# Order and size of attention's loads, and the order in which the attention result is split, in a one-layer encoder step

## The reference, cut to what matters

```
h = rmsnorm(x) * (1 + scale) + shift            # shift, scale, gate from silu(c) @ w_ada + b_ada
q, k, v, indexer, z_a, z_b, g_a, g_b = split(h @ w_in)     # q, k get a per-head RMS norm
att_a = attention over the top-k keys that an indexer picks (8 heads, 2 kv heads, dim 64)
att_b = attention over own chunk of 64 and 2 before it, with a sink per head
o_a = (att_a * silu(z_a)) @ w_oa ;  o_b = (att_b * silu(z_b)) @ w_ob
y = x + gate * ((sigmoid(g_a) * o_a + sigmoid(g_b) * o_b) @ w_out)
```

## Time and profile before

| | |
|---|---|
| time before, median of 3 (lowest to highest) | 1013.48 us (1010.45 to 1014.51) |
| the profiled execution's own time | 1018.09 us |
| its span, first to last instruction | 1016.3 us |
| PE busy / weight loads busy | 959.4 us (94%) / 855.6 us (84%) |
| DVE / ACT / POOL busy | 652.5 us (64%) / 392.3 us (39%) / 375.1 us (37%) |
| mean granted TensorE clock | 0.973 of full |
| DMA | 126.40 MB, 124 GB/s on the mean |

### The profile page before, as it was taken

One profiled execution on the slowest core, in us unless ns is written; L12 is line 12 of the kernel. 1 busy time (PEld: TensorE's weight loads), 2 busy tenths in 40 slices (PEclk: granted clock), 3 DMA queues, 4 the chain that ended last, 5 costly groups with the idle time before them and its releaser, 6 DMA issues. The chain is left out here.

```text
span 1016.3 us, 17645 instructions
## 1 busy us (share of the span) xinstructions
PE 959.4 (94%) x6482; PEld 855.6 (84%) x6482; DVE 652.5 (64%) x1375; ACT 392.3 (39%) x1166; POOL 375.1 (37%) x420
## 2 busy tenths in 40 slices
PE   4859999999999999999999888999999889999998
PEld 2558887878789999999999666778777679999998
DVE  6563365999999999999980575766665553331111
ACT  5664566444422322122111555666665522212100
POOL 0261113212253533121243477655631145537332
PEclk9878999999999999999999798999999899999999
DMA  9820013643461323232132834423334665534332
GB/s 319 305 73 28 25 34 108 227 162 94 141 205 59 115 82 108 81 107 76 63 136 71 252 97 139 140 91 102 96 102 111 196 189 163 152 93 139 101 121 73
DMA packets 112187, 126.40 MB, mean 124 GB/s; under 512 B 12105, under 2 KB 89305, under 8 KB 111978
## 3 DMA queue, kind: packets, MB, share of 16 engines
q1 hardware_dynamic: 101698, 114.30, 36.2%
q10 hardware_dynamic: 10408, 11.01, 3.5%
HBM read 95.49 MB, written 35.75 MB: 129 GB/s over the span
## 5 line engine op out<-in xcount | busy, mean ns | idle before, releaser
L1569 PE MATMUL PS<-HH,WH 128*128 128x384 f32 (+1 forms) x576 | 188.8, 328 | 0.0
L1571 PE MATMUL PS<-HH,WL 128*128 128x384 f32 (+1 forms) x576 | 187.9, 326 | 0.0
L1570 PE MATMUL PS<-HL,WH 128*128 128x384 f32 (+1 forms) x576 | 187.7, 326 | 0.0
L1404 DVE MAX8 M<-SC 128x8 f32<-128x384 f32 (+3 forms) x210 | 174.8, 870 | 11.6 <-DVE SC L1409 11.0
L1409 DVE MATCH_REPLACE8 SC<-M,SC 128x384 f32<-128x384 f32 (+3 forms) x210 | 179.9, 864 | 0.0
L880 POOL TENSOR_TENSOR WL<-RAW,WH 128x512 fp32r<-128x512 f32 x72 | 94.2, 1312 | 182.0 <-ACT WH L1031 182.0
L1569 PE MATMUL PS<-WH,HH 128*128 128x512 f32 (+3 forms) x288 | 111.1, 386 | 8.6 <-DVE HL L1348 8.5
L1569 PEld LDWEIGHTS PS<-HH,WH 128*128 128x128 f32 x576 | 108.1, 188 | 3.8 <-issue 3.7
L1570 PE MATMUL PS<-WL,HH 128*128 128x512 f32 (+3 forms) x288 | 109.0, 378 | 0.0
L1571 PE MATMUL PS<-WH,HL 128*128 128x512 f32 (+3 forms) x288 | 108.7, 377 | 0.0
L1570 PEld LDWEIGHTS PS<-HL,WH 128*128 128x128 f32 x576 | 108.1, 188 | 0.0
(11 more groups left out here) (202 smaller groups left out, 1967.4 us busy)
## 6 DMA issues: line engine op xcount, KB each, us to landing
RAW<-in_w_all SPq DMA_DIRECT2D x72, 256.0 KB, 2.7
gz<-STG SPq DMA_DIRECT2D x48, 192.0 KB, 1.8
WADA<-in_w_ada SPq DMA_DIRECT2D x16, 512.0 KB, 12.3
snat<-STG SPq DMA_DIRECT2D x24, 256.0 KB, 2.0
QKV<-snat SPq DMA_DIRECT2D x8, 768.0 KB, 5.7
GT<-gz SPq DMA_DIRECT2D x32, 192.0 KB, 2.5
XN<-in_x_prompt SPq DMA_DIRECT2D x8, 512.0 KB, 6.1
btad<-bvd ACTq DMA_DIRECT2D x4, 1024.0 KB
```

What stands on the lines that cost most here:

```text
L1404: V.max(M8[0:r, a, :], w).then_inc(sel_step, 1)
L1569: T.matmul(out, wh, mh, start=first, stop=False)
L1570: T.matmul(out, wh, ml, start=False, stop=False)
L1571: return T.matmul(out, wl, mh, start=False, stop=last)
```

## The change

Four things. (1) Of attention's first loads only `BTB` and `VB` stay ahead of the loop; `BTA`'s first piece and `VA` go to SP's step 1, the six loads for the sample to step 9, and the gate of group 0 is loaded at step -1 instead of 4. (2) A tile's `QKV` is loaded 14 steps ahead instead of 7. (3) The rest of `BTA` comes in two pieces of 256 and 512 columns (1 MB and 2 MB), issued by ScalarE at steps 13 and 36, instead of six pieces of 128 columns issued by SP at steps 13, 35, 51, 67, 83 and 99. (4) `AZ` has both halves of column group 0 first; ScalarE's third high part moves from step 137 to 139, and DVE's second, third and fourth low part are made at step 139 and behind the loop, where the second was at step 135 and the third at 139.

```
--- before.py
+++ after.py
@@ -408,7 +408,7 @@
         U8 = 16 * SAMPLE
         GEND = [max(u for u, x in enumerate(UNITS) if x[:2] == (g // 2, g % 2)) + 1 for g in range(2 * NT)]
 
-        AZ = [(0, 0), (1, 0), (0, 1), (1, 1), (2, 0), (2, 1)]
+        AZ = [(0, 0), (0, 1), (1, 0), (1, 1), (2, 0), (2, 1)]
 
         def nh(tt):
 
@@ -463,11 +463,10 @@
         assert all(TQ[n][1] == ("Q", 0, n) for n in range(EARLY_T))
         PREP0 = {16 * (tt - 1): tt for tt in range(NT)}
         CACHE_STEP = {16 * (2 + i): i for i in range(5)}
-        LOAD_AT, NORM_AT, SPLIT_AT = -7, -5, 2
+        LOAD_AT, NORM_AT, SPLIT_AT = -14, -5, 2
         RD_AT, RB_AT, FIN_AT = ({GEND[g] + d: g for g in range(2 * NT)} for d in (1, 4, 4))
         ZR_AT, OUT_AT = ({GEND[g] + (d if g < 2 * NT - 1 else e): g for g in range(2 * NT)} for d, e in ((8, 6), (9, 7)))
-        BT_AT = {13 if tt == 2 else 16 * (tt - 1) + 3: tt for tt in range(2, SAMPLE)}
-        ZT_AT = {GEND[g] + (2 if g == 2 * NT - 1 else 0 if g // 2 == SAMPLE else -4): g for g in range(2 * NT)}
+        ZT_AT = {GEND[g] + (2 if g == 2 * NT - 1 else 0 if g // 2 == SAMPLE else -9 if g == 0 else -4): g for g in range(2 * NT)}
         SINK_AT = {GEND[2 * tt + 1]: tt for tt in range(NT)}
 
         def prep(s, after):
@@ -717,13 +716,6 @@
 
             sp.dma_start(BTB[:], btbd).then_inc(kvb_in, 16)
             sp.dma_start(VB[:], vp[:, :, 1408:1536]).then_inc(kvb_in, 16)
-            sp.dma_start(BTA[:, :, 768:1024], btad[:, :, 768:1024]).then_inc(kvc_in, 16)
-            sp.dma_start(VA[:], vp[:, :, 640:768]).then_inc(kvc_in, 16)
-            for dst, src in ((CK[:, 0:4, :], t["cache_ak"].rearrange("(n p) c -> p n c", p=128)), (CK[:, 4, :], t["cache_bk"]),
-                             (VAS[:, 0:4, :], t["cache_av"].rearrange("(n p) c -> p n c", p=128)),
-                             (VAS[0:DEC, 4, :], snat[SEQ:TOK, 640:768]),
-                             (VBS[:, 0, :], t["cache_bv"]), (VBS[0:DEC, 1, :], snat[SEQ:TOK, 1408:1536])):
-                sp.dma_start(dst, src).then_inc(rest_in, 16)
             for i in range(3):
                 sp.wait_ge(stg_out[i], 16 * NST[i])
             wo_v = t["w_o"].rearrange("(k p) n -> p k n", p=128)
@@ -748,11 +740,15 @@
                 if s == NU + 1:
                     sp.wait_ge(exp_done, NU)
                     g_load(0)
-                if s in BT_AT:
-                    tt = BT_AT[s]
-                    if tt >= 3:
-                        sp.wait_ge(min_done, 16 * (tt - 1) + 1)
-                    sp.dma_start(BTA[:, :, 896 - 128 * tt:1024 - 128 * tt], btad[:, :, 896 - 128 * tt:1024 - 128 * tt]).then_inc(bta_in, 16)
+                if s == 1:
+                    sp.dma_start(BTA[:, :, 768:1024], btad[:, :, 768:1024]).then_inc(kvc_in, 16)
+                    sp.dma_start(VA[:], vp[:, :, 640:768]).then_inc(kvc_in, 16)
+                if s == 9:
+                    for dst, src in ((CK[:, 0:4, :], t["cache_ak"].rearrange("(n p) c -> p n c", p=128)), (CK[:, 4, :], t["cache_bk"]),
+                                     (VAS[:, 0:4, :], t["cache_av"].rearrange("(n p) c -> p n c", p=128)),
+                                     (VAS[0:DEC, 4, :], snat[SEQ:TOK, 640:768]),
+                                     (VBS[:, 0, :], t["cache_bv"]), (VBS[0:DEC, 1, :], snat[SEQ:TOK, 1408:1536])):
+                        sp.dma_start(dst, src).then_inc(rest_in, 16)
                 tt = prep(s, LOAD_AT)
                 if tt is not None and tt >= 2:
                     sp.wait_ge(xg_ready, tt - 1)
@@ -1190,6 +1186,11 @@
                 nc.scalar.dma_start(ZST[g][:], attd.rearrange("(k p) n -> p k n", p=128)[:, :, g0:g0 + gn]).then_inc(z_in[g], 16)
 
             for s in range(S0, S1):
+                if s in (13, 36):
+                    c = slice(512, 768) if s == 13 else slice(0, 512)
+                    if s == 36:
+                        act.wait_ge(min_done, 33)
+                    nc.scalar.dma_start(BTA[:, :, c], btad[:, :, c]).then_inc(bta_in, 16)
                 if s == U8 - 12:
                     act.wait_ge(xg_ready, NT)
                     z_load(0)
@@ -1243,7 +1244,7 @@
                     tt = SINK_AT[s]
                     act.wait_ge(sink_sum, tt + 1)
                     nc.scalar.activation(ES[:, 0, :], SD[:], ACT.Exp).then_inc(sink_act, 1)
-                if s == NU + 1:
+                if s == NU + 3:
                     act.wait_ge(min_done, NU)
                     attention_high(2)
                 if s in CACHE_STEP:
@@ -1473,8 +1474,8 @@
                     link(V.memset(BTB[CHUNK:128, :, 0:64], NEG_BIG))
                 if s == 16:
                     dve.wait_ge(kvc_in, 32)
-                if s % 16 == 0 and 32 <= s < U8:
-                    dve.wait_ge(bta_in, 16 * (s // 16 - 1))
+                if s in (32, 64):
+                    dve.wait_ge(bta_in, 16 * (s // 32))
                 if s == U8:
                     dve.wait_ge(btp_in[0], 32)
                 if s == GEND[2 * SAMPLE]:
@@ -1528,12 +1529,11 @@
                 if s == U8 + 2:
                     dve.wait_ge(qk_pe, U8 - 8)
                     attention_low(0)
-                if s == U8 + 7:
-                    attention_low(1)
                 if s == NU + 3:
                     dve.wait_ge(qk_pe, NU)
-                    attention_low(2)
-
+                    attention_low(1)
+
+            attention_low(2)
             dve.wait_ge(zr_done, 2 * SAMPLE)
             attention_low(3)
             for i in range(3 * KD):
```

More of the change, by code:

```diff
@@ L719, in _ @@
             sp.dma_start(VB[:], vp[:, :, 1408:1536]).then_inc(kvb_in, 16)
[L720 to L726, removed]
             for i in range(3):
```

2 lines of the change are left out of this document (1 added, 1 removed).

## The result

| | before | changed |
|---|---|---|
| median of 6 runs each, us | 1011.93 (1009.87 to 1014.51) | 1022.54 (1020.36 to 1023.93) |
| ratio, 95% interval | | 1.010 (1.0075 to 1.0124) |
| profiled execution: time, span, us | 1018.09, 1016.3 | 1023.80, 1022.0 |
| mean granted clock of PE | 0.973 | 0.973 |

The forecast was 1011.5 with a range of 1006.5 to 1015.0. The two profiled executions differ by 5.7 us only, because the one of before took 4.6 us more than the median that it was forecast from. Against that one the changed kernel lost 10.4 us of span, which is what the medians say, so I read the changed trace against both.

A forecast was written before the change was run, and what follows sets the result against it. PE (94% busy) was taken as the bound, with gains only in its idle or slow time. Terms 0 - 1.5 + 0 - 0.2 = -1.7, plus -0.3 for a shorter half-clock stall, took 1013.5 to 1011.5 us, range 1006.5 to 1015.0.

The forecast's parts named there:

- `BTA` in larger pieces on ScalarE's queue: Attention's later bias loads: pieces arrive hidden, delays to SP's trips fit the slack; 0 us, issue cost bounded 0 to +1.2.
- rival 3: Step 36's 2 MB holds SP's trips of groups 3 and 4, making tile 4's keys late: +3.6, 1017.1 us; chance 0.09.
- First loads: Attention's start: PE's 2.46 us wait stays, `XG` of tile 2 starts about 578.0; 0 us, bounds -0.5 and +0.5.
- Tile 3's keys: POOL's keys before tile 3: `QKV` leaves the queue ahead of `attd`, so they end 1.5 us sooner; bounds 0 and 3.1.
- The join: Attention to o-projection: last attention products end sooner, second product idles about 5 us; -0.2 us, bounds -1.7 and +2.0.
- The rule of the Trainium skill: SP's round trips in attention: pieces off SP's row would shorten them, and the sum would hold with more slack.
- rival 1: Tile 3's stall nearly vanishes: -3.1, clock stays up with under 1 us of stall: -2.5, join -0.2; 1007.7 us; chance 0.22.

The follow-up runs named there:

- 1: Kernel before with only the rest of `BTA` in two pieces (1 MB, 2 MB) issued by ScalarE at steps 13 and 36: 1017.93 us, 1.0051.
- 5: Changed kernel with the bias table back in six 512 KB pieces on SP's queue: 1014.75 us, 1.0019 to the unchanged kernel.
- 2: Kernel before with only the first loads reordered and `QKV` loaded 14 steps ahead: 1012.18 us, 1.0000.
- 6: Kernel before with its six 512 KB `BTA` pieces at their old steps, issued by ScalarE instead of SP: 1013.83 us, 1.0013.
- 7: Kernel before with `BTA` in two large pieces (1 MB at step 13, 2 MB at step 36), issued by SP: 1016.59 us, 1.0038.
- 9: Changed kernel with the split order of before: 1020.90 us, 1.0070 to the unchanged kernel.
- 10: Kernel before with the two large `BTA` pieces on ScalarE's queue and `QKV` 14 steps ahead, first loads as before: 1019.60 us, 1.0062.
- 11: Kernel before with the two large `BTA` pieces on ScalarE's queue and the first loads reordered, `QKV` 7 steps ahead: 1018.46 us, 1.0049.
- second profile: The kernel before, unchanged, profiled a second time: 1013.45 us in the one run, span 1011.6.
- 3: Kernel before with only the new order of the splits: 1015.88 us, 1.0026.
- 8: Kernel before with the new split order, but DVE's third low part at step 139, ahead of the multiply of group 17: 1012.59 us, 1.0009.

## Why the prediction was wrong

**The failed step is the term "`BTA` in larger pieces on ScalarE's queue", put at 0; by itself it measured +5.2 us (1), and together with the rest about +8 (5).** "The pieces themselves are due at steps 32 and 64 and come 20 steps ahead: hidden" was right for the pieces. The price of what they do to SP's trips was wrong. I took the cost to SP's trips as 3.1 us each, from the one trip that the profile showed beside another large transfer (`ZST` and `ORAW`, 2.5 MB, issued on ScalarE's queue from 786.75 on), against 3.4 us of slack at tile 4, and for group 0 "+0.5 ... contained above". Measured, the wait isn't a fixed price: it grows with what is in flight. POOL's multiply of group 0, where POOL waited for it, came 5.7 us (2) and 6.1 us (6) after the issue of a 512 KB piece, and 6.9 to 8.6 us (1, 7, 9, 10, 11, full change) after that of 1 MB, within about 1 us of that piece's landing in the five of them whose trace gives it. For group 3 the tie to the landing is looser: its multiply started 3.7 us ahead of the landing of the 2 MB (11) to 3.8 behind it (7). Its trip took 9.7 to 12.6 us beside 2 MB and 6.8 to 7.6 in the unchanged kernel. In the full change that is 4.9 to 5.8 us more, in a place where 3.4 could be taken.

**This is rival 3, with the chance 0.09.** Its mechanism and place were right in the full change and in 9: the 2 MB of step 36, group 3's trip, tile 4's keys, then half clock behind the stall. It priced two trips at 3.1 us, 6.2 in all; one trip took nearly that, group 4's little. The stall before tile 4 is 3.38 us where the rival had 2.8, and the stretch to tile 8 took 2.4 us more, where it had 2.5 for the clock. It gave 1017.1, and the time was 1022.5. What I held against it, POOL's idle time first, is not slack when group 4's trip, behind whose multiply the keys are made, starts behind group 3's. And I gave it one place; there were more. The 1 MB at step 13 met group 0, and in 1, 10 and 11 the delay came out as POOL's `XNB` beside DVE's `SD`, which neither the forecast nor a rival had.

**First loads: 0, and right.** `XG` started at 575.0, which by attention's start is 577.4 of the first profile, forecast 578; PE's wait before 573 shrank from 2.46 to 2.05. The addition at 584.85 took 0.17 us as forecast, but this confirms nothing, as it did so in the unchanged kernel's second profile. The first loads and the early `QKV` together (2) are 1.0000; the first loads alone weren't run.

**Tile 3's keys, -1.5: not seen in the time.** Without the large pieces (2) they end 51.7 us after attention's start, against 52.6 to 54.0 in the four profiles whose program is the same as before up to there (both of before, 3, 8), so the gain may be there. In the full change they end at 617.60, and that is 55.7: later and not sooner, because group 0's trip was held. And the stall that the gain was to shorten stood in one execution of the unchanged kernel and not in the next. A gain read from one stall of one profile holds only if the stall is a fixture. The 2.9 us by which tile 4 comes sooner in 2 lie mostly within what those four profiles differ by (76.5 to 80.6), so there is no gain to look for at the end.

**The join, -0.2: its steps right, its size +2.6 (3), off by 2.8.** This is the second term that failed. The idle time before the second product (6.74 us, forecast 5), its releaser and the half clock for the first matmuls are as forecast. What I held them against was again one execution: in the first profile of before the third product ran at half clock for its first half (5.9 us for its 24 matmuls), in the second at full clock (4.3). Followed from SP's issue of `RB` of group 15 (800.72, before 796.95), the fourth product starts after 28.1 us, before after 27.8 and 25.9; it is 28.1 to 28.6 in the three kernels with the new order and DVE's late low part (full change, 3, 5) and 25.9 to 27.8 in the nine profiles with the old order and its low parts as before. The rest stands behind the seventh product: 1.6 us at half clock behind a stall that every kernel has. In the windows of 840 to 848 of the changed kernel:

```profile
840.00:844.00 4.00, 2.13 (x11) 1.92 (x10) 2.09 (x3) 1.42 (x2) 2.99 (x3) 0.94 0.94 341
844.00:848.00 4.00, 4.00 (x17) 4.00 (x17) 0.00 (x0) 0.00 (x0) 2.27 (x1) 0.64 0.72 212
```

The clock fell there in all three kernels that idle 6 us or more before the second product (3, 5, the full change), and, of the eleven other profiles, in that of 11 alone (0.81 and 0.77). So the 6 us are no necessary condition, and one profile each can't make them a sufficient one. That the long wait costs the time is what 3 against 8 points to (1.0026 and 1.0009), but their intervals overlap; by way of which stretch of clock, the traces only suggest.

**The rule of the Trainium skill** that I had weighed ("DMA: Bandwidth & Descriptors", section "Queues, rings and completion order") says that a DMA engine round-robins between the rows of SP and ACT. From it I had hoped for shorter trips with the pieces off SP's row. The traces hardly bear that hope out: group 3's trip took 11.1 us beside ScalarE's 2 MB (1) and 11.4 behind SP's own (7). In 11 the 4 KB store did get through in 1.9 us, issued 0.2 us behind the 2 MB, but the load after it then took the wait. So a small transfer in a row of its own was not reliably kept from the load.

**What stays open.** The parts make 5.2 + 0 + 2.6 = 7.8 us, the whole 10.1. The 2.3 us between them are of the size of the intervals. The traces show where they could be. All kernels with the 2 MB piece reach tile 4 late (80.8 to 84.4, without it 75.8 to 80.6), but by two ways. In 1, 10 and 11 PE waits for DVE 14 us ahead of tile 4, pays the half clock there, and finds the keys ready. In the full change and in 9 that wait is short (1.04 and 0.83 us), PE waits at tile 4 for the keys (3.38 and 2.94 us), and from 646 to 652 it is busy at half clock; from tile 4 to tile 8 they take 2.3 to 2.7 us more than 1, 10 and 11. Experiment 7 has a stall of 2.18 us at tile 4 and takes 1.5 to 1.8 more. Which way a kernel goes depends on where POOL's `XNB` falls beside DVE's `SD`, a matter of 1 to 2 us; with one profile of each, whether it goes the same way every time isn't shown.

## What to carry to other kernels

Where a chain contains small round trips through DRAM, bound the amount that may be in flight at one moment: here a piece of 512 KB cost such a trip little, and one of 1 or 2 MB cost it 2 to 6 us, on either queue. Fewer and larger issues gained nothing here, as the issuing queue wasn't what waited. A prefetch's own due time says nothing about this; ask which small transfer is issued while it flies, who stands behind that, and what its delay moves beside what. And before a stall is counted as gain, profile the unchanged kernel twice.

## What the runs showed of the hardware

- The same short stall can be free or cost half clock: the 1.87 us on PE before the seventh product left the granted clock at 1.00 in ten profiles; in four it fell, to 0.64, 0.65 and 0.71 over four microseconds (full change, 3, 5) and to 0.81 and 0.77 over eight (11). The 3.29 us before tile 2 left it at 1.00 in the full change, and 3.33 us at the same place in 9 were followed by 0.57 over four microseconds (598.58 to 602.58). So a stall's price can't be read from its length, and rival 1's condition (less than 1 us of stall, and the clock stays up) is no line that these traces draw.
- A DVE addition whose operands are both in SBUF can last until POOL's operation beside it ends. Two of 8 numbers per partition, 0.16 us by themselves, did so: the one of 2.14 us in the kernel before, which took 0.17 us here, clear of POOL, and `SD` of 2.33, 2.30 and 1.77 us in 1, 10 and 11, each ending within 0.05 us of `XNB`. `TM` at 820.76, 0.56 us in most places, took 2.39 us, to 823.15; POOL's `WOL` ran from 820.36 to 822.73.
- The half clock at the start of attention ended at about 576 in the second profile of before and at about 589 in that of 3, whose program is the same up to there: such a stretch can differ by over 10 us between executions without any edit.
